# Twelve spare slots for the next expert's gate and first up slices, copied to the ring by ScalarE and VectorE

## The reference

```
logits = xt @ w_router + b_router
top_vals, top_idx = lax.top_k(logits, TOP_K)          # 4 of 32 experts for each of 512 tokens
top_gates = jax.nn.softmax(top_vals, axis=-1)
def expert_block(args):
    xb, e = args
    gate = jnp.minimum(xb @ w_gate[e] + b_gate[e], SWIGLU_LIMIT)
    up = jnp.clip(xb @ w_up[e] + b_up[e], -SWIGLU_LIMIT, SWIGLU_LIMIT)
    glu = gate * jax.nn.sigmoid(SWIGLU_ALPHA * gate)
    return (glu * (up + 1.0)) @ w_down[e] + b_down[e]
```

## Time and profile before

| | us |
|---|---|
| median of 3 runs | 2937.39 |
| the profiled execution's own time | 2935.62 |
| its span, first to last instruction | 2933.9 |
| first `gc` of the expert loop | 1751.95 |
| last `gc` of the expert loop (block 49) | 2883.31 |
| TensorE busy | 2772.3 (94%) |
| VectorE busy | 1529.7 (52%) |
| ScalarE busy | 956.0 (33%) |

### The profile page before, as it was taken

One profiled execution on the slowest core, in us unless ns is written; L12 is line 12 of the kernel. 1 busy time (PEld: TensorE's weight loads), 2 busy tenths in 40 slices (PEclk: granted clock), 3 DMA queues, 4 the chain that ended last, 5 costly groups with the idle time before them and its releaser, 6 DMA issues.

```text
span 2933.9 us, 38779 instructions
## 1 busy us (share of the span) xinstructions
PE 2772.3 (94%) x12664; PEld 1659.5 (57%) x12664; DVE 1529.7 (52%) x3078; ACT 956.0 (33%) x1805; POOL 116.1 (4%) x171
## 2 busy tenths in 40 slices
...
DMA  8271246864323035342323079689899789899897
GB/s 268 72 215 42 89 130 185 238 185 130 94 86 86 15 86 171 95 119 79 97 73 106 1 279 409 267 349 410 319 410 409 297 322 410 319 410 410 326 407 285
DMA packets 398912, 638.18 MB, mean 218 GB/s; under 512 B 34576, under 2 KB 284560, under 8 KB 398816
## 3 DMA queue, kind: packets, MB, share of 16 engines
...
...
## 4 chain that ended last, share of the span: by engine, by line
PE 73%; DMA 9%; SPq 5%; DVE 5%; ACT 4%; issue 2%; POOL 0%; ACTq 0%; DVEq 0%; POOLq 0%
PE bank L2620 24%; PE bank L196 14%; PE bank L198 14%; PE bank L197 13%; DMA ring<-w_down 6%; SPq L2430 4%; DMA ring<-w_gate 2%; PE bank L1084 1%; PE bank L1125 1%; PE bank L1085 1%; DVE WLO L167 1%; ACT WHI L157 1%; PE bank L2614 1%; PE bank L1118 0%; ACT la L411 0%
## 5 line engine op out<-in xcount | busy, mean ns | idle before, releaser
L2620 PE MATMUL bank<-ring,xT 128*64 128x512 f32 x3200 | 728.8, 597 | 24.6 <-DMA ring<-w_up 12.7
L196 PE MATMUL bank<-HH,WHI 128*128 128x512 f32 x1344 | 540.2, 402 | 34.5 <-DVE WLO L167 17.3
L197 PE MATMUL bank<-HL,WHI 128*128 128x512 f32 x1344 | 529.9, 394 | 0.0
L198 PE MATMUL bank<-HH,WLO 128*128 128x512 f32 x1344 | 529.6, 394 | 0.0
L2620 PEld LDWEIGHTS bank<-ring,xT 128*64 128x64 f32 x3200 | 220.3, 137 | 496.8 <-issue 363.0
L2620 PE MATMUL bank<-ring,hT 128*64 128x512 f32 x1600 | 372.5, 601 | 26.1 <-DMA ring<-w_down 26.1
L167 DVE TENSOR_TENSOR WLO<-RAW,WHI 128x2048 fp32r<-128x2048 f32 (+1 forms) x132 | 281.6, 2134 | 105.7 <-ACT WHI L157 105.5
L196 PEld LDWEIGHTS bank<-HH,WHI 128*128 128x128 f32 x1344 | 256.8, 191 | 98.4 <-DVE WLO L167 23.0
L157 ACT ACTIVATE WHI<-RAW 128x2048 fp32r<-128x2048 f32 (+1 forms) x132 | 234.6, 1777 | 165.0 <-PE bank L198 129.7
L197 PEld LDWEIGHTS bank<-HL,WHI 128*128 128x128 f32 x1344 | 256.7, 191 | 55.5 <-issue 2.9
L198 PEld LDWEIGHTS bank<-HH,WLO 128*128 128x128 f32 x1344 | 256.3, 191 | 54.6
...
## 6 DMA issues: line engine op xcount, KB each, us to landing
ring<-w_gate SPq DMA_DIRECT2D x256, 512.0 KB, 9.4
ring<-w_up SPq DMA_DIRECT2D x256, 512.0 KB, 15.5
ring<-w_down SPq DMA_DIRECT2D x256, 512.0 KB, 15.1
...
```

The costliest lines, as they stand in the source:

```text
L196: pe.matmul(out, lhi, rhi, start=start, stop=False)
L197: pe.matmul(out, lhi, rlo, start=False, stop=False)
L198: return pe.matmul(out, llo, rhi, start=False, stop=stop)
L2620: ins = pe.matmul(out[halves(h), :], xT[:, k % 4, halves(k // 4)], m["ring"][:, c, h * 512:(h + 1) * 512], start=False, stop=k == KD - 1)
```

## The change

`ring` becomes `slots`, with 39 slots: 0 to 11 are staging slots, 15 to 38 are the old ring (`RING_SLOT` = 15). The gate slices and the first four up slices (`STAGED` = 12) are no longer loaded into the ring. SyncE loads them into the staging slots for the expert that comes next, in the iteration of an expert's first block (`turnover`), once this block's copies have emptied them (`taken`). In every block ScalarE copies slots 0 to 7 and VectorE 8 to 11 to the ring: from the staging slots in an expert's first block, and from the ring slot to itself in an extra block (`from`, `level`). TensorE waits for `taken` in place of `raw` for these twelve. Routing works out four more rows of numbers per block (`nxt`, `turnover`, `from`, `level`), `n2x` is built behind `tokcol` instead of ahead of it, TensorE waits for the first gather directly, and SyncE starts its loop after `nexts`, `stored` and `picked`.

```diff
@@ -2132,7 +2132,8 @@
 MOE_CHUNKS = [(w, k) for w in ("gate", "up", "down") for k in range(KD)]
 UP_FROM, DOWN_FROM = KD, 2 * KD
-MOE_SIGNALS = "mo_gain mo_end mo_last mo_first0 mo_first1 mo_first2 mo_act mo_dve mo_pe mo_down mo_idx mo_x mo_y " + " ".join(f"mo_raw{c}" for c in range(MOE_SLOTS))
+STAGED, RING_SLOT = 12, 15
+MOE_SIGNALS = "mo_gain mo_end mo_last mo_first0 mo_first1 mo_first2 mo_act mo_dve mo_pe mo_down mo_taken mo_idx mo_x mo_y " + " ".join(f"mo_raw{c}" for c in range(STAGED, MOE_SLOTS)) + "".join(f" mo_st{c}" for c in range(STAGED))
 MOE_SEEDED = ("mo_act", "mo_dve", "mo_pe", "mo_down", "mo_x", "mo_y")
...
@@ -2180,6 +2181,10 @@
                 sp.wait_ge(*mix.event("logits"))
             moe_load(sp, m, W, c, 0).then_inc(mo.sem[f"mo_first{c // KD}"], 16)
         sp.wait_ge(*sg.event("bei"))
+        for c in range(STAGED):
+            sp.wait_ge(*sg.event("nexts")).then_inc(mo.sem[f"mo_st{c}"], 16)
+        sp.wait_ge(*sg.event("stored"))
+        sp.wait_ge(*sg.event("picked"))
         return
...
+        v.wait_ge(*sg.event("cmp"))
+        v.tensor_scalar(m["cmp3"][:], m["i48"][0:32, :], m["prevc"][:], None, ALU.is_ge).then_inc(*sg.inc("ro_dve", also=[("cmp3", None)]))
...
@@ -2318,10 +2328,25 @@
         v.wait_ge(*sg.last("ro_step"))
         v.tensor_scalar(m["sel"][:], m["pmb"][:], m["bef"][0:96, 0:1], None, ALU.is_equal)
         v.memset(m["seld"][:], 0.0)
+        v.wait_ge(*sg.event("tokens"))
+        v.tensor_scalar(m["tokcol"][:], b[7][:, 0:NB + 1], vec[:, V2_HALF:V2_HALF + 1], None, ALU.add).then_inc(*sg.inc("ro_dve", also=[("tokcol", None)]))
         for k in range(KD):
             v.tensor_scalar(m["n2x"][:, k % 4, k // 4 * BLK:(k // 4 + 1) * BLK], one[:, 0:BLK], vec[:, V2_N2 + k:V2_N2 + k + 1], None, ALU.mult)
-        v.wait_ge(*sg.event("tokens"))
-        v.tensor_scalar(m["tokcol"][:], b[7][:, 0:NB + 1], vec[:, V2_HALF:V2_HALF + 1], None, ALU.add).then_inc(*sg.inc("ro_dve", also=[("tokcol", None)]))
+        nextf, heldf = m["nextf"][:, 1:NB], m["heldf"][:, 0:NB]
+        v.wait_ge(*sg.event("nextp"))
+        v.tensor_copy(m["nextf"][:, 0:NB], b[6][0:1, 336:336 + NB]).then_inc(*sg.inc("ro_step"))
+        v.wait_ge(*sg.last("ro_step"))
+        v.tensor_copy(m["nxt"][:, 0:NB], m["nextf"][:, 0:NB])
+        v.memset(m["heldf"][:, 0:1], 1.0)
+        v.tensor_tensor(m["heldf"][:, 1:NB], nextf, m["nextf"][:, 0:NB - 1], ALU.not_equal).then_inc(*sg.inc("ro_step"))
+        v.wait_ge(*sg.last("ro_step"))
+        v.tensor_tensor_scan(m["ordf"][:, 0:NB], one[0:1, 0:NB], heldf, 0.0, ALU.mult, ALU.add).then_inc(*sg.inc("ro_step"))
+        v.wait_ge(*sg.last("ro_step"))
+        v.tensor_scalar(m["level"][:, 0:NB], m["ordf"][:, 0:NB], 16.0, None, ALU.mult)
+        v.tensor_scalar(m["from"][:, 0:NB], heldf, -float(RING_SLOT), float(RING_SLOT), ALU.mult, ALU.add)
+        v.tensor_tensor(heldf, heldf, m["nextf"][:, 0:NB], ALU.mult).then_inc(*sg.inc("ro_step"))
+        v.wait_ge(*sg.last("ro_step"))
+        v.tensor_scalar(m["turnover"][:, 0:NB], heldf, 1.0, None, ALU.min).then_inc(*sg.inc("ro_dve", also=[("nexts", None)]))
         v.wait_ge(*sg.event("gexp"))
         v.reciprocal(m["gs"][:], m["gs"][:]).then_inc(*sg.inc("ro_step"))
...
         pe.matmul(b[5][:, 256:256 + NB + 1], m["ord"][:, 66:67].broadcast_to([32, P]), m["cmp2"][:], start=False, stop=True).then_inc(*sg.inc("ro_pe", also=[("bep", None)]))
+        pe.wait_ge(*sg.event("cmp3"))
+        pe.matmul(b[6][0:1, 336:336 + NB + 1], m["ord"][:, 65:66], m["cmp3"][:], start=True, stop=False)
+        pe.matmul(b[6][0:1, 336:336 + NB + 1], m["ord"][:, 66:67], m["cmp"][:], start=False, stop=True).then_inc(*sg.inc("ro_pe", also=[("nextp", None)]))
         pe.wait_ge(*sg.event("ohb"))
         for n in range(16):
             pe.wait_ge(*sg.event("ohp", n))
...
@@ -2436,7 +2463,7 @@
         return moe_load(sp, m, W, c, e)
     def preloaded(c):
-        if c % KD == 0:
+        if c in (STAGED, DOWN_FROM):
             sp.wait_ge(sg.sem[f"mo_first{c // KD}"], 16 * KD)
     def loads(i, experts, fresh, chunks):
@@ -2452,9 +2479,21 @@
                 preloaded(c)
                 sp.wait_ge(*sg.event("used", c, loop=i, back=1)).then_inc(sg.sem[f"mo_raw{c}"], 16)
+    def staged(i):
+
+        e = sp.value_load(m["nxt"][0:1, bass.ds(i, 1)], min_val=0, max_val=EXPERTS - 1)
+        turnover = sp.value_load(m["turnover"][0:1, bass.ds(i, 1)], min_val=0, max_val=1)
+        with sp.If(turnover == 1):
+            for c in range(STAGED):
+                sp.wait_ge(*sg.event("taken", c, loop=i, back=1))
+                moe_load(sp, m, W, c, e, 0).then_inc(sg.sem[f"mo_st{c}"], 16)
+        sp.wait_ge(*sg.event("taken", UP_FROM - 1, loop=i, back=1)).then_inc(sg.sem["mo_taken"], 1)
+        sp.wait_ge(*sg.event("taken", STAGED - 1, loop=i, back=1)).then_inc(sg.sem["mo_taken"], 1)
+
     with sp.Fori(0, count) as i:
-        loads(i, "bei", "fresh", range(0, DOWN_FROM))
+        loads(i, "bei", "fresh", range(STAGED, DOWN_FROM))
         loads(i, "bed", "freshd", range(DOWN_FROM, MOE_SLOTS))
+        staged(i)
     sp.wait_ge(sg.sem["mo_y"], count * 32).then_inc(sg.sem["mo_end"], 1)
     sp.wait_ge(*sg.event("g", loop=count, back=1)).then_inc(sg.sem["mo_end"], 1)
...
+def held_at(eng, m, i):
+
+    return (eng.value_load(m["from"][0:1, bass.ds(i, 1)], min_val=0, max_val=RING_SLOT),
+            eng.value_load(m["level"][0:1, bass.ds(i, 1)], min_val=16, max_val=16 * EXPERTS))
+
+
+def taken_from(m, c, first):
+
+    return m["slots"][:, bass.ds(first + c, 1), :].rearrange("p o n -> p (o n)")
+
+
 def moe_act(act, sg, fi, m, b, W, count):
     def store(i, h):
@@ -2503,7 +2553,17 @@
         act.wait_ge(*sg.event("gathered", loop=i, back=1))
         for piece in QUADRANTS[:1] if last else QUADRANTS:
             ins = act.activation(by_features(m["xr"], *piece), by_rows(m["xg"], *piece), ACT.Copy)
-        ins.then_inc(*done("xr"))
+        if last:
+            ins.then_inc(sg.sem["mo_act"], 1 + UP_FROM)
+        else:
+            ins.then_inc(*done("xr"))
+
+        if not last:
+            first, level = held_at(act, m, i)
+            act.wait_ge(*sg.event("g", loop=i, back=1))
+            for c in range(UP_FROM):
+                act.wait_ge(sg.sem[f"mo_st{c}"], level)
+                act.activation(m["slots"][:, RING_SLOT + c, :], taken_from(m, c, first), ACT.Copy).then_inc(*sg.inc("mo_act", also=[("taken", c)]))
...
@@ -2561,7 +2621,13 @@
         ins.then_inc(*done("hh"))
         v.wait_ge(*sg.event("hh", loop=i, back=1))
         v.wait_ge(*sg.event("y", loop=i, back=1))
-        v.transpose(m["hT"][:].rearrange("p k n -> p (k n)"), m["hh"][:]).then_inc(*done("hT"))
+        v.transpose(m["hT"][:].rearrange("p k n -> p (k n)"), m["hh"][:]).then_inc(*((sg.sem["mo_dve"], 1 + STAGED - UP_FROM) if last else done("hT")))
+
+        if not last:
+            first, level = held_at(v, m, i)
+            for c in range(UP_FROM, STAGED):
+                v.wait_ge(sg.sem[f"mo_st{c}"], level)
+                v.tensor_copy(m["slots"][:, RING_SLOT + c, :], taken_from(m, c, first)).then_inc(*sg.inc("mo_dve", also=[("taken", c)]))
         v.wait_ge(*sg.event("seld_used", loop=i, back=1))
         v.tensor_scalar(m["seld"][:], m["pmb"][:], m["bef"][0:96, bass.ds(i - 1, 1)], None,
...
+            ins = pe.matmul(out[halves(h), :], xT[:, k % 4, halves(k // 4)], m["slots"][:, RING_SLOT + c, h * 512:(h + 1) * 512], start=False, stop=k == KD - 1)
         return ins
+
+    def ready(c, i, first):
+
+        if c >= STAGED:
+            pe.wait_ge(*sg.event("raw", c, loop=i))
+        elif first:
+            pe.wait_ge(sg.sem[f"mo_first{c // KD}"], 16 * KD)
+        else:
+            pe.wait_ge(*sg.event("taken", c, loop=i, back=1))
...
-            pe.wait_ge(*sg.event("raw", c, loop=i))
+            ready(c, i, first)
             products(c, b[0], m["xT"]).then_inc(*done(("used", c), *[("g", None)] * (c == UP_FROM - 1)))
         pe.wait_ge(*sg.event("uc", loop=i, back=1))
         bias(b[1], m["sel"][:], 1)
         for c in range(UP_FROM, DOWN_FROM):
-            pe.wait_ge(*sg.event("raw", c, loop=i))
...
```

More of the change, by code:

```diff
@@ L2204, in route_program @@
         ins.then_inc(*sg.inc("ro_act", "gexp", also=[("gexp", None)]))
+        act.wait_ge(*sg.event("nexts"))
         act.wait_ge(*sg.event("picked"))
@@ L2266, in route_program @@
         v.wait_ge(*sg.event("places"))
+        v.tensor_scalar(m["behind"][:], b[5][0:32, 208:240], pos, 1.0, ALU.subtract, ALU.is_equal)
         v.tensor_scalar(grid, b[5][0:32, 208:240], pos, None, ALU.is_gt).then_inc(*sg.inc("ro_dve", also=[("ahead", None)]))
@@ L2393, in route_program @@
         pe.matmul(b[5][0:32, 200:201], m["grid"][:], m["nbf"][:], start=True, stop=True)
+        pe.matmul(b[5][0:32, 201:202], m["behind"][:], m["nbf"][:], start=True, stop=True)
```

(16 more changed lines are left out.)

14 lines of the change are left out of this document (11 added, 3 removed).

## The result

The changed kernel took 2967.09 us (median of 4 runs, 2964.88 to 2968.01), the one before 2936.98 in the same session: ratio 1.0098, 95% interval [1.008, 1.0115]. It is slower by 30 us, where +20 was forecast and 2975 was the range's upper end. The profiled execution of the changed kernel took 2966.39, span 2964.7.

A forecast was written before the change was run, and what follows sets the result against it. Expert-stage waits for slices (95 us) were taken as the winnable loss, set by when stretches start and slice order. Loop terms 13.6 + 4.6 - 0.8 = +17.4, plus 3 for copies and restarts, made +20: 2937.39 to 2957 us, range 2940 to 2975.

The forecast's parts named there:

- Start: In SyncE's queue after extra blocks, the first load would be up slot 12, starting a full-DMA stretch 9.6 us later.
- hole: Behind a stretch's first four up slices, SyncE's waits on down slots would leave DMA idle about 5 us.
- order: Twelve staged slices for the next stretch stand before block 14's down slices, giving back the 15.4 us in hand.
- D(14)'s last slice: Last down slice for block 14, forecast to land at 2097.6 us, against 2084.1 wanted without any stall.
- Middle stretches: Four inner stretches of full DMA in the expert loop: +3.4 us each, 13.6 together, plus 0.5 a stretch for copies and restarts.
- The first stretch: Full DMA from the loop's beginning, twelve slices more and no head start: loses 6.3 us, +4.6 with the routing.
- plus 2 for a later start: Term in the first full-DMA stretch's end: 2 us for starting later, giving an end at 1897.4.
- The routing's 3.5 us: Routing ahead of the loop: moved and added instructions delay block 0's gate products by 3.5 us.
- The copies: ScalarE's and VectorE's slot copies: hidden in unstalled blocks, at 1.05 and 0.85 us (bound 1.28) each.
- A: Rival in the expert loop: staged slices fill idle DMA time, six stretches gain 10 us each, -60, 2877; 8%.
- B: Rival at each stretch's beginning: late first load and idle gap cost less, about 0 each, 2938 to 2942; 8%.
- C: Rival in ScalarE's blocks: copies pace the stage; at 1.6 us a copy, +64 on the forecast, 3021; 9%.

The follow-up runs named there:

- e_order: Changed kernel, but where an extra block follows, the staged slices load one iteration later, behind the current expert's down slices; 2934.44 us, 0.9993 of the kernel before.
- the pair of eight and twelve slots: Changed kernel with both load-order edits, with eight staged slices (2921.45 us) or twelve (2915.52 us).
- tables_late: Changed kernel with the chain making the staged loads' tables moved behind the routing's picks and gates; 2961.93 us, 1.0087 of the kernel before.
- thin_copies: Changed kernel with each of a block's twelve copies moving 64 of 1024 columns, waits and loads unchanged; 2965.82 us, 1.0095 of the kernel before.
- after: The changed kernel itself, first trace; the profiled execution took 2966.39 us.
- changed_again: The changed kernel run once more, word for word, giving its second trace; 2965.90 us, 1.0093 of the kernel before.
- e_hole: Changed kernel with SyncE issuing staged slices before the down-slot waits where those load nothing; 2943.34 us, 1.0025 of the kernel before.
- e_tail: Changed kernel with the final gathers held until the last down slice of block 48 has landed; 2964.48 us, 1.0096 of the kernel before.
- two_orders: Changed kernel with staged slices one iteration later before extra blocks, and ahead of down-slot waits that load nothing; 2915.52 us, 0.9928 of the kernel before.

## Why the prediction was right, and where its sizes were off

**Start, hole and order: right, and each shown.** The late first load and the staged issue came within 0.3 us of the forecast, D(14)'s last slice too. Mending the hole gives 24 us back and the order 33; both together 51.6, less than the 56 of the two. In the middle stretches the two add up almost fully (37.3 us together, 15.0 and 23.0 one by one); what is missing lies behind the loop, where each edit alone had its rest shorter by 4.0 and 5.6 and both together by 4.6. So 4 to 6 us of each single figure lie where neither the hole nor the order was expected to act, and where two traces of the changed kernel differ by 3.2. The prediction's sentence that the head start "is thus given back before the extra blocks begin" is what e_order and the pair of eight and twelve slots bear out.

**Middle stretches: +3.4 and 0.5 forecast, 3.6 to 5.1 measured.** Close. The hole was 4 us instead of 5. The last wait is where it was said to be, but more of the loss lies ahead of it, at D(11), as the section on the result shows.

**The first stretch has one term too small, and a remainder: +5.1 forecast (4.6 and 0.5), +9.7 measured, 12.2 in the second trace.** The term that was too small is "plus 2 for a later start". SyncE waits for the transposes of `tk`, and then passes six register loads and the twelve waits of block 0's slots before it comes to the staged slices:

```profile
1751.13 4.68 SPq L2457 DMA_DIRECT2D slots<-w_gate  x8
```

The first gate load of before:

```profile
1747.44 4.97 SPq L2430 DMA_DIRECT2D ring<-w_gate  x8
```

The new one is 3.7 us behind it, 5.9 in the second trace, and DMA stayed full until 1901 (0.78 of the window from 1898 to 1902) instead of 1897.4. The stretch lost 176.4 - 164.8 = 11.6 us, where 6.3 were forecast. DMA's late end is 3.7 of these 5.3, and the start 1.7 of the 3.7; what the remainder is made of isn't shown. The routing's 3.5 us (3.35 measured) are right as a delay of G(0), and in the prediction's sum they cancel: they make the wanted time later and the loss smaller by as much as they add. What the routing costs passes through the queue, in the term for the start. So the rival that the expectation of tables_late calls the prediction's own term isn't in the prediction.

**Left out altogether: the rest behind the loop,** 1.6 to 4.9 us. The sum has no term for what lies behind block 49. Of the 10.3 us that the first trace lies above the sum (30.7 against 20.4), 4.9 are here and 4.6 in the first stretch.

**The copies: hidden, as forecast.** ScalarE's took 1.05 us as the row of that size had it, at a pitch of 0.96, and the register pair ahead of them cost nothing that shows: `xr` ended at 1938.06 and the copies began at 1938.08.

```profile
1932.96 5.10 ACT L2555 ACTIVATE xr<-xg 32x128 f32<-32x128 f32 x16
...
1938.08 7.69 ACT L2566 ACTIVATE slots<-slots 128x1024 f32 x8
```

VectorE's took 0.69, below both bounds that I drew (0.85 and 1.28), because the 427 ns of the nearest row, a cast of 512 elements, were doubled with their fixed part in them. thin_copies shows it: 64 columns took 195 ns and 1024 took 690, which is 0.52 ns a column and some 160 ns that don't grow with the size; 512 columns come to 426 by these, and the cast's row has 427. The Trainium skill (VectorE: DVE Perf Modes, "The perf-mode tier table (the rule you actually need)") lists an fp32 copy in SBUF at the double rate; with the 150 cycles of fixed part that its section "The TRN2 errata" gives, that is (150 + 512) / 0.96 GHz = 690 ns, an estimate from the page that this row meets. The rule on the port pair that the prediction weighed was not put to the test: in none of eight traces (after, changed_again, e_order, e_hole, e_tail, tables_late, thin_copies, two_orders) does a gather's issue in the loop fall on a copy of VectorE, and the longest took 1.01 us.

**Rivals.** A (staged slices fill idle time) needed the order turned round, as its own condition said; with the order and the hole mended the six stretches lose 24 us less than before (from the table), of the 60 that it named. B fell: the hole and the start of the middle stretches cost what they were said to. C fell with thin_copies.
